# Two hybrid encoder layers on one core: the opening's order of loads, and the layer-0 modulation divided between TensorE and VectorE

## The chip, the cores and the metric

One Trainium2 chip, one core. The time is device microseconds of the launch, as the median of several runs; smaller is better. The trace is of one profiled execution. TensorE (PE) multiplies, VectorE (DVE), ScalarE (ACT) and GpSimd (POOL) work elementwise, and SyncE (SP) issues most transfers.

## What is computed

Two consecutive layers on x of 512 tokens by 1024 channels, in float32. Everything before the layers' first projection matters here:

```python
c_act = jax.nn.silu(c)
for l in range(DEPTH):
    mod = c_act @ w_ada[l] + b_ada[l]
    shift, scale, gate = jnp.split(mod, 3, axis=-1)
    h = _rmsnorm(x, norm_w) * (1.0 + scale[:, None]) + shift[:, None]
    proj = h @ w_in
...
    x = x + gate[:, None] * (merged @ w_out[l])
```

The projection feeds a windowed attention, a pooling branch and a state-space branch, whose sum goes through w_out; a final RMSNorm ends the program. Shift and scale of layer 0 take 2048 of the 3072 columns of `c_act @ w_ada[0]`.

## The kernel before

Channels lie on partitions: xT, h and the products are 8 tiles of 128 channels by 512 tokens (k = 0 to 7). Each weight tile is 1024 by 128. A float32 product is made of three rounded ones: the tile is split into a high part (`w_hi`, on ScalarE) and a low part (`w_lo`, on GpSimd), h likewise (h_hi on ScalarE, h_lo on VectorE), and TensorE adds hi*hi, hi*lo and lo*hi for each k: 24 products of 128x128 by 128x512 for one weight tile, all with float32r operands. The order on each engine is written out by hand, and engines wait for each other through counting semaphores. SyncE issues transfers in program order, so a transfer queued behind a waiting one waits too.

The opening does the following, all of it in layer 0.

- **Transfers** (`sync`, L304 on): c, then the first quarter of w_ada (`quarter(0)`, L308 to L317), the four blocks of x, two weight tiles of w_in, and then by turns quarters 1, 2 and 3 and the other weight tiles. A quarter is 256 columns of shift and 256 of scale for all 1024 rows: eight transfers of 256 KB into one of two buffers, zs for quarters 0 and 2, big for 1 and 3. Weight tiles go whole, 512 KB each. Small tables (biases, norms, conv weights; `s_rows`) are issued by ScalarE (L899 to L903).
- **Modulation** (VectorE, `use_quarter`, L1139 to L1151): for each of eight row blocks k, the 128x512 slab times silu(c) of that block, added to a sum in psC1. The eighth goes to `quarter_acc`. TensorE then adds over the partitions (`quarter_sums`, L589 to L595, a product with a vector of ones for each 128 columns), and `quarter_mod` adds bias and makes the gain.
- **x**: TensorE transposes it block by block (`x_rows`, L579 to L587), VectorE or ScalarE copies it to xT; ScalarE squares it, VectorE forms the inverse root, and TensorE copies that over all partitions (`spread`, L568 to L573).
- **h**: quarter q gives h tiles 2q and 2q+1: `h_32` (VectorE), `h_high` (ScalarE), `h_low` (VectorE), one after the other.
- **Wide part** (TensorE, `wide_part`, L613 to L624, and the list after L626): five weight tiles (`WIDE`: the three pairs' first five) are multiplied side by side in five PSUM banks, two k at a time, as h tiles appear. After it come small tables and the sixth tile, and from then on weight tiles two by two.

Of the kernel before, what the change touches and what calls it, by code (L numbers as in the profile page):

```python
# [103 lines left out]
def build(nc, x, c, w_ada, b_ada, norm_w, w_in, rel_bias, attn_sinks, pool_w, pool_scale, conv_w, conv_b, dt_bias,  # L104
# [11 lines left out]
    with ExitStack() as ctx:  # L116
# [75 lines left out]
        s_rawx = [sem(f"raw_wide_loaded{i}") for i in range(4)]  # L192
# [13 lines left out]
        s_adau = sem("ada_used")  # L206
        s_adam, s_mod = sem("ada_summed"), sem("mod_done")
# [65 lines left out]
        quarter_acc = [buf_d[:, 0:512], buf_d[:, 512:1024]]  # L273
        quarter_ps = [main[1]] + [psB[:, 512:1024]] * (QUARTERS - 1)
# [14 lines left out]
        def part_count(l, u, half):  # L289

            return (l * COUPLES + u) * 2 + half + 1

        def wait_raw(eng, l, u, b):
            if is_wide(l, u):
                eng.wait_ge(s_rawx[2 * u + b - 2], 16)
            else:
                eng.wait_ge(s_raw[b], (l * COUPLES + u + 1 - (2 if l + u > 0 else 0)) * 16)
# [7 lines left out]
        def _(sp):  # L305
            sp.dma_start(stage_e[0:KT, :], c.rearrange("b (a p) -> (b a) p", p=P)).then_inc(s_crow, 16)

            def quarter(q):  # L308

                n = D // QUARTERS  # L310
                for g in range(KT // 2):
                    if q >= 2:
                        sp.wait_ge(s_adau, (q - 2) * KT + 2 * g + 2)
# [11 lines left out]
            def load(l, u, b, w, col, kt=KT):  # L325
                if is_wide(l, u):
                    sp.dma_start(w_bufs(l, u, b)[0], w[l, :, :, col:col + P]).then_inc(s_rawx[2 * u + b - 2], 16)
                    return
                sp.wait_ge(s_split[b], part_count(0, 0, 1) if (l, u) == (0, 3) else (l * COUPLES + u) * 2)
                sp.dma_start(raw[:, b, 0:kt, :], w[l, :, 0:kt, col:col + P]).then_inc(s_raw[b], 16)  # L330

            def wide(i):
                load(0, i // 2, i % 2, w_in_t, i * P + COL_Q)

            quarter(0)
# [31 lines left out]
            for l in range(DEPTH):  # L367
# [63 lines left out]
                def next_slab(l, half, k):  # L431
                    n = half * KT + k
                    if l + 1 < DEPTH:
                        sp.wait_ge(s_yz, (l + 1) * PAIRS)
                        if n >= 4:
                            sp.wait_ge(s_adau, QUARTERS * KT + n - 3)
# [18 lines left out]
        def _(pool):  # L455
# [20 lines left out]
            def split_half(l, u, b, half, kt=KT):  # L476
                raw_b, hi_b, lo_b = w_bufs(l, u, b)
                cut = slice(half * BT_, (half + 1) * BT_)
                pool.wait_ge(s_hi[b], part_count(l, u, half) if kt == KT else (l * COUPLES + u) * 2 + 2)
# [12 lines left out]
            for l in range(DEPTH):  # L492
                for u in range(U_GA + 1):
                    split(l, u, 0)
                    split(l, u, 1)
# [20 lines left out]
        def _(pe):  # L516
# [18 lines left out]
            def tile_part(l, u, b, k0, k1, ready):  # L535
# [3 lines left out]
                for k in range(k0, k1):  # L539
                    pe.wait_ge(s_split[b], part_count(l, u, k // BT_))  # L540
# [37 lines left out]
            pe.wait_ge(s_rows, 16 * N_ROWS)  # L578
# [961 lines left out]
```

## Time and profile before

| | |
|---|---|
| median of 3 runs | 1195.08 us (1193.89 to 1195.45) |
| the profiled execution | 1194.21 us |
| its span in the trace | 1192.5 us |
| TensorE busy | 1145.6 us, 96% of the span |
| VectorE, ScalarE, GpSimd busy | 628.8, 514.0, 519.5 us |
| moved by DMA | 139.22 MB |

The span leaves out what lies around the program in the measured time (1.7 us here). The chain of waits follows back, from the last instruction, what released each step; the timeline lists instructions with start and duration. TensorE's durations overlap: the distance between two starts is what one costs in a row of them.

### The profile page before, as it was taken

The page shows a single profiled execution, that of the slowest core. Times are in us where ns is not written, and L with a number is a line of the kernel's source. Part 1 is how long each engine was busy: PE and PEld are TensorE (multiplying, and loading weights), DVE is VectorE, ACT ScalarE, POOL GpSimd, SP SyncE. Part 2 cuts the span into 40 slices and gives each one's busy share as a digit, 9 for nine tenths or more (in the row PEclk, how much of TensorE's full clock was granted, in tenths as well). Part 3 has the DMA queues.
Part 4 walks back from the last instruction along what each step waited for, and adds up shares of the span by engine and source line. Part 5 has one row for each costly group of instructions (what it writes and reads, how often), then busy time and mean ns, then how long its engine had stood idle before and what let it go on. Part 6 is the DMA issues. An engine that isn't in the chain of part 4 may idle for free.

```text
span 1192.5 us, 15180 instructions
## 1 busy us (share of the span) xinstructions
PE 1145.6 (96%) x5882; PEld 939.5 (79%) x5882; DVE 628.8 (53%) x759; ACT 514.0 (43%) x879; POOL 519.5 (44%) x381
## 2 busy tenths in 40 slices
PE   4899999999999999999979999999999999999997
PEld 3678888878888888887867788888888887788876
DVE  5806256568786554445340444555877753132274
ACT  4235256755445523224233534656444553232322
POOL 2334534434334446554514463434343425455441
PEclk9899999999999999999979999999999999999998
DMA  9745523335433455543313462332634422433332
GB/s 301 201 100 168 168 58 89 89 99 129 115 107 82 132 170 157 155 129 105 109 35 98 133 214 72 90 88 69 162 88 107 122 73 80 115 100 95 92 93 81
DMA packets 222200, 139.22 MB, mean 117 GB/s; under 512 B 11912, under 2 KB 212656, under 8 KB 222128
## 3 DMA queue, kind: packets, MB, share of 16 engines
q1 hardware_dynamic: 221480, 137.59, 40.5%
q8 instruction: 47, 0.77, 0.3%
q10 hardware_dynamic: 648, 0.66, 0.2%
q14 instruction: 25, 0.20, 0.1%
HBM read 135.08 MB, written 2.62 MB: 115 GB/s over the span
## 4 chain that ended last, share of the span: by engine, by line
PE 85%; DVE 5%; DMA 4%; POOL 2%; ACT 1%; SPq 1%; issue 1%; DVEq 0%; ACTq 0%
PE main L519 74%; DMA raw<-in_w_in 4%; PE psC L519 3%; PE psA L519 3%; PE psB L519 2%; POOL w_lo L480 2%; DVE h_lo L1463 1%; DVE xbc L1418 1%; ACT w_hi L864 1%; SPq L428 1%; DMA xbc<-in_x 1%; PE psB L674 1%; PE psB L694 0%; DVE psC L1150 0%; DVE misc L1298 0%
## 5 line engine op out<-in xcount | busy, mean ns | idle before, releaser
L480 POOL TENSOR_TENSOR w_lo<-raw,w_hi 128x512 fp32r<-128x512 f32 x352 | 503.9, 1454 | 639.1 <-ACT w_hi L864 639.1
L519 PE MATMUL main<-h_hi,w_hi 128*128 128x512 f32 x1152 | 461.1, 400 | 16.0 <-POOL w_lo L480 7.4
L519 PE MATMUL main<-h_hi,w_lo 128*128 128x512 f32 x1152 | 450.8, 391 | 0.0
L519 PE MATMUL main<-h_lo,w_hi 128*128 128x512 f32 x1152 | 450.7, 391 | 0.0
L864 ACT ACTIVATE w_hi<-raw 128x512 fp32r<-128x512 f32 x352 | 204.2, 625 | 343.2 <-PE main L519 247.8
L519 PEld LDWEIGHTS main<-h_hi,w_hi 128*128 128x128 f32 x1152 | 217.6, 189 | 75.8 <-issue 25.6
L519 PEld LDWEIGHTS main<-h_hi,w_lo 128*128 128x128 f32 x1152 | 217.6, 189 | 46.6
L519 PEld LDWEIGHTS main<-h_lo,w_hi 128*128 128x128 f32 x1152 | 217.8, 189 | 45.0 <-issue 1.9
L1452 DVE TENSOR_TENSOR tmp<-main,misc 128x512 f32<-128x512 f32 x32 | 22.1, 691 | 174.8 <-PE main L519 171.1
L1298 DVE SCALAR_TENSOR_TENSOR misc<-main,cols,misc 128x511 f32<-128x511 f32 (+2 forms) x96 | 71.9, 749 | 65.1 <-ACT misc L864 62.5
L519 PE MATMUL main<-y_hi,w_hi 128*128 128x512 f32 x256 | 101.3, 396 | 0.0
L519 PE MATMUL main<-y_lo,w_hi 128*128 128x512 f32 x256 | 99.7, 389 | 0.0
L519 PE MATMUL main<-y_hi,w_lo 128*128 128x512 f32 x256 | 99.7, 389 | 0.0
L864 ACT ACT_TABLE_LOAD x69 | 88.5, 1283 | 2.0 <-PEq L1526 0.8
L864 ACT ACTIVATE misc<-main 128x512 f32<-128x512 f32 x48 | 28.6, 597 | 139.1 <-PE main L519 139.0
L519 PEld LDWEIGHTS main<-y_hi,w_hi 128*128 128x128 f32 x256 | 48.1, 188 | 10.8 <-issue 1.4
L519 PEld LDWEIGHTS main<-y_hi,w_lo 128*128 128x128 f32 x256 | 48.1, 188 | 10.2
L519 PEld LDWEIGHTS main<-y_lo,w_hi 128*128 128x128 f32 x256 | 48.1, 188 | 9.5
L1272 DVE SCALAR_TENSOR_TENSOR xbc<-xbc,fcol 128x1024 f32<-128x1024 f32 x16 | 26.8, 1674 | 27.2 <-DMA xbc<-in_w_ada 27.1
L1454 DVE TENSOR_TENSOR big<-big,tmp 128x512 f32<-128x512 f32 x32 | 38.8, 1213 | 1.1
L864 ACT ACTIVATE misc<-main,cols 128x512 f32<-128x512 f32 x32 | 24.6, 769 | 25.5 <-PE main L519 25.5
L1242 DVE TENSOR_SCALAR tmp<-psC,hpar 16x512 f32<-16x512 f32 x2 | 1.5, 740 | 62.4 <-PE psC L519 62.4
(225 smaller groups left out, 1078.4 us busy)
## 6 DMA issues: line engine op xcount, KB each, us to landing
raw<-in_w_in SPq DMA_DIRECT2D x128, 512.0 KB, 3.8
xbc<-in_w_ada SPq DMA_DIRECT2D x16, 512.0 KB, 4.8
zs<-in_w_ada SPq DMA_DIRECT2D x16, 512.0 KB, 4.7
raw<-in_w_pc SPq DMA_DIRECT2D x16, 512.0 KB, 3.8
raw<-in_w_out SPq DMA_DIRECT2D x16, 512.0 KB, 3.7
zs<-in_w_ada SPq DMA_DIRECT2D x16, 256.0 KB, 5.6
big<-in_w_ada SPq DMA_DIRECT2D x16, 256.0 KB, 6.2
tmp<-step_rows SPq DMA_DIRECT2D x8, 512.0 KB, 4.1
```

Source lines behind the costliest of these rows:

```text
L428: sp.dma_start(buf_w[e * CHUNK:(e + 1) * CHUNK, :].rearrange("q (i n) -> q i n", n=PAIR), bass.AP(tensor=exp_rows.tensor, offset=first, ap ...
L480: nc.gpsimd.tensor_tensor(lo_b[:, cut, :], raw_b[:, cut, :], hi_b[:, cut, :].bitcast(F32), ALU.subtract).then_inc(s_split[b], 2 * BT_ // kt)
L519: return nc.tensor.matmul(o, a, b_, start=start, stop=stop)
L674: last = nc.tensor.transpose(psB[:, h * P:(h + 1) * P], buf_d[:, h * P:(h + 1) * P], ident[:, :])
L864: return nc.scalar.activation(o, i, func, **kw)
L1242: ch.link(ts_(v, psC0[0:SH, :], hpar[:, 0, l:l + 1], None, ALU.add))
L1272: stt(gate_acc, gate_slab[b], fcol[:, ds(j * 2 + b, 1)], gate_acc, ALU.mult, ALU.add).then_inc(s_gsu[b], 1)
L1298: ins = stt(cvb[:, b, back:SEQ], main[b][:, 0:SEQ - back], lcol[:, col_at(p * 4 + (V_CW + tap * CT + i))], cvb[:, b, back:SEQ], ALU.mult, ...
L1418: last = stt(xbc[:, i, tok], xbc[:, i, tok], gskip[:, i:i + 1], y_sum[:, i * P:(i + 1) * P], ALU.mult, ALU.add)
L1452: tt(buf_r[:, 0:512], main[1][:, :], gate, ALU.mult).then_inc(s_evac[1], 1)
L1454: tt(at(merged, m), at(merged, m), buf_r[:, 0:512], ALU.add).then_inc(s_acc, 1)
L1463: tt(at(h_lo, k), at(merged, k), at(h_hi, k).bitcast(F32), ALU.subtract).then_inc(s_m, 1)
```

## The change

Seven edits, all in the opening of layer 0 (the other hunks renumber semaphores).

1. SyncE sends the four blocks of x first, then quarter 0.
2. The five wide weight tiles go in halves of 256 KB (k 0 to 3 of all five between quarters 0 and 1, k 4 to 7 of all five between quarters 1 and 2). The sixth follows quarter 3. Quarter 2 waits for TensorE's use of quarter 0 instead of VectorE's.
3. Quarters 0 and 2 are formed on TensorE (`quarter_rows`): silu(c) of row block k, one column, is stationary, the 128x512 slab moves, and eight such float32 products add up a row of 512 in PSUM. ScalarE copies the row (`row_copy`), and four products with a one turn it into columns (`quarter_cols`). VectorE keeps quarters 1 and 3.
4. TensorE transposes all of x before quarter 0; it waits for the small tables after two of the four blocks, not before the first.
5. The wide part runs over five tiles at once in each of its four passes (before: four, with the fifth put in behind the sums).
6. The eight products of quarter 2 stand in the second pass, four behind the second weight tile and four behind the fourth.
7. ScalarE and GpSimd split the wide tiles by halves in the order in which they arrive.

```diff
-                        sp.wait_ge(s_adau, (q - 2) * KT + 2 * g + 2)
+                        sp.wait_ge(s_adar if q == 2 else s_adau, 2 * g + 2)
...
+            def wide(half):
+                cut = slice(half * BT_, (half + 1) * BT_)
+                for i, (u, b) in enumerate(WIDE):
+                    sp.dma_start(w_bufs(0, u, b)[0][:, cut, :], w_in_t[0, :, cut, i * P:(i + 1) * P]
+                                 ).then_inc(s_rawx[i + 6 * half], 16)
             for t in range(PAIRS):
                 sp.dma_start(stage_x[:, t, :], x_t[:, t, :]).then_inc(s_xrow[t], 16)
+            quarter(0)
             wide(0)
+            quarter(1)
             wide(1)
-            quarter(1)
-            wide(2)
-            wide(3)
             quarter(2)
-            wide(4)
             quarter(3)
-            wide(5)
+            sp.dma_start(w_bufs(0, 2, 1)[0], w_in_t[0, :, :, 5 * P:6 * P]).then_inc(s_rawx[5], 16)
...
+                if l == 0:
+                    for half in range(2):
+                        for u, b in WIDE:
+                            split_half(l, u, b, half)
+                    split(l, 2, 1)
+                for u in range(U_GA if l == 0 else 0, U_GA + 1):
...
-            pe.wait_ge(s_rows, 16 * N_ROWS)
...
+            row_ps = [psC1[0:1, :], psB[0:1, 512:1024]]
+            def quarter_rows(q, k0, k1):
+                for k in range(k0, k1):
+                    pe.wait_ge(s_ada[q % 2 * 4 + k // 2], (q // 2 + 1) * 32)
+                    mm(row_ps[q // 2], fcol[:, k:k + 1], quarter_slab[q % 2][:, k], k == 0, k == KT - 1
+                       ).then_inc(s_adar, 1)
+            def quarter_cols(q):
+                pe.wait_ge(s_arow, q // 2 + 1)
+                for j in range(QUARTERS):
+                    last = mm(quarter_ps[q][:, q * QUARTERS + j:q * QUARTERS + j + 1],
+                              quarter_row[q // 2][:, j * P:(j + 1) * P], ones[0:1, 0:1])
+                last.then_inc(s_adam, 1)
...
             x_rows(0)
+            x_rows(1)
+            pe.wait_ge(s_rows, 16 * N_ROWS)
             for l in range(DEPTH):
                 nc.tensor.transpose(psC0[:, l * P:l * P + V_ROWS], stage_v[0:V_ROWS, l, :],
                                     ident[0:V_ROWS, 0:V_ROWS])
             nc.tensor.transpose(psC0[:, 2 * P:2 * P + 2 * KT], stage_e[0:2 * KT, :],
                                 ident[0:2 * KT, 0:2 * KT]).then_inc(s_rT, 1)
-            quarter_sums(0)
-            for t in range(1, PAIRS):
-                x_rows(t)
+            x_rows(2)
+            x_rows(3)
+            pe.wait_ge(s_cact, 1)
+            quarter_rows(0, 0, 6)
             pe.wait_ge(s_cols, 2)
             spread(psC0, rms, 1)
-            for i in range(2):
+            quarter_rows(0, 6, 8)
+            quarter_cols(0)
+            for i in range(5):
+                if i == 2:
+                    pe.wait_ge(s_xc, PAIRS)
                 wide_part(i, 0, 2)
-            pe.wait_ge(s_xc, PAIRS)
             quarter_sums(1)
-            for i in range(2, 4):
-                wide_part(i, 0, 2)
-            for i in range(4):
+            for i in range(5):
                 wide_part(i, 2, 4)
-            quarter_sums(2)
-            wide_part(4, 0, 4)
-            for i in range(4):
+                if i == 1:
+                    quarter_rows(2, 0, 4)
+                if i == 3:
+                    quarter_rows(2, 4, 8)
+            quarter_cols(2)
+            for i in range(5):
                 wide_part(i, 4, 6)
-            quarter_sums(3)
-            wide_part(4, 4, 6)
+                if i == 2:
+                    quarter_sums(3)
             for i in range(5):
                 wide_part(i, 6, 8)
...
+            def row_copy(i):
+                act.wait_ge(s_adar, (i + 1) * KT)
+                f(quarter_row[i], (psC1[0:1, :], psB[0:1, 512:1024])[i], ACT.Copy).then_inc(s_arow, 1)
+            row_copy(0)
             for b in range(2):
                 w_hi_half(0, 0, b, 0)
             h_high(0, 0)
             h_high(0, 1)
-            for b in range(2):
-                w_hi_half(0, 0, b, 1)
-            w_hi_part(0, 1, 0)
-            w_hi_part(0, 1, 1)
+            for u, b in WIDE[2:]:
+                w_hi_half(0, u, b, 0)
+            for u, b in WIDE[:4]:
+                w_hi_half(0, u, b, 1)
             h_high(0, 2)
             h_high(0, 3)
-            w_hi_part(0, 2, 0)
+            w_hi_half(0, 2, 0, 1)
+            row_copy(1)
             h_high(0, 4)
             h_high(0, 5)
...
             dve.wait_ge(s_cact, 1)
-            for k in range(KT):
-                use_quarter(0, k)
             x_copy(0)
+            x_copy(1)
+            inverse_root(rms, s_xsq, PAIRS, 1, sm[:, 4])
             dve.wait_ge(s_rT, 1)
             nc.vector.tensor_copy(cols[:, :, :], psC0[:, 0:2 * P].rearrange("p (l n) -> p l n", l=DEPTH)
                                   [:, :, 0:V_ROWS]).then_inc(s_cols, 1)
             nc.vector.tensor_copy(fcol[:, KT:2 * KT], psC0[:, 2 * P + KT:2 * P + 2 * KT]).then_inc(s_cols, 1)
+            x_copy(2)
             dve.wait_ge(s_cols, 2)
-            x_copy(1)
-            quarter_mod(0)
-            x_copy(2)
-            inverse_root(rms, s_xsq, PAIRS, 1, sm[:, 4])
-            for q in range(QUARTERS):
-                if q > 0:
-                    for k in range(0 if q == 1 else 2, KT):
-                        use_quarter(q, k)
-                    if q < QUARTERS - 1:
-                        for k in range(2):
-                            use_quarter(q + 1, k)
-                    quarter_mod(q)
+            def two_tiles(q):
+                quarter_mod(q)
                 if q == 0:
                     dve.wait_ge(rms[3], 1)
                     dve.wait_ge(s_xc, PAIRS)
...
                 h_32(0, 2 * q + 1)
                 h_low(0, 2 * q)
                 h_low(0, 2 * q + 1)
+            two_tiles(0)
+            for k in range(KT):
+                use_quarter(1, k)
+            two_tiles(1)
+            for k in range(2):
+                use_quarter(3, k)
+            two_tiles(2)
+            for k in range(2, KT):
+                use_quarter(3, k)
+            two_tiles(3)
```

TensorE, the program's start, up to the first product of the wide part. In these rows `zs,fcol` is slab by silu(c), `ident,xbc` a transpose of x, `ones,tmp` the sums or the turn into columns, `ident,sm` the spread of the inverse root, `w_hi` and `w_lo` a weight tile. Before:

```order
L585 MATMUL psA<-ident,xbc 128x128 x8
L628 MATMUL psC<-ident,big 128x124 x2
L630 MATMUL psC<-ident,big 128x16
L519 MATMUL main<-ones,tmp 128x1 x4
L585 MATMUL psB<-ident,xbc 128x128 x8
L585 MATMUL psA<-ident,xbc 128x128 x8
L585 MATMUL psB<-ident,xbc 128x128 x8
L519 MATMUL psC<-ident,sm 128x128 x4
L519 MATMUL main<-h_hi,w_hi 128x512
```

The same place in the changed kernel:

```order
L593 MATMUL psA<-ident,xbc 128x128 x8
L593 MATMUL psB<-ident,xbc 128x128 x8
L655 MATMUL psC<-ident,big 128x124 x2
L657 MATMUL psC<-ident,big 128x16
L593 MATMUL psA<-ident,xbc 128x128 x8
L593 MATMUL psB<-ident,xbc 128x128 x8
L527 MATMUL psC<-zs,fcol 1x512 x6
L527 MATMUL psC<-ident,sm 128x128 x4
L527 MATMUL psC<-zs,fcol 1x512 x2
L527 MATMUL main<-ones,tmp 128x1 x4
L527 MATMUL main<-h_hi,w_hi 128x512
```

Eight products of 1x512 now stand between the transposes and the columns, the spread among them.

TensorE in the wide part's second pass, where it goes from tile 1 (bank main) to tile 2 (bank psA). Here `y_hi` and `y_lo` are the split parts of wide tiles 2 to 4. Before:

```order
L519 MATMUL main<-h_hi,w_hi 128x512
L519 MATMUL main<-h_lo,w_hi 128x512
L519 MATMUL main<-h_hi,w_lo 128x512
L519 MATMUL psA<-h_hi,y_hi 128x512
L519 MATMUL psA<-h_lo,y_hi 128x512
```

The same place in the changed kernel:

```order
L527 MATMUL main<-h_hi,w_hi 128x512
L527 MATMUL main<-h_lo,w_hi 128x512
L527 MATMUL main<-h_hi,w_lo 128x512
L527 MATMUL psB<-zs,fcol 1x512 x4
L527 MATMUL psA<-h_hi,y_hi 128x512
L527 MATMUL psA<-h_lo,y_hi 128x512
```

Four products of quarter 2 stand between the two tiles; the other four stand between psA and psB of the same pass.

VectorE, from h tiles 0 and 1 to the modulation of tiles 2 and 3. `tmp<-xT` is h_32, `psC<-big` and `psC<-zs` are uses of a slab, `mod<-psB` is `quarter_mod`. Before:

```order
L1178 SCALAR_TENSOR_TENSOR tmp<-xT,mod,psC 128x512 x2
L1182 SCALAR_TENSOR_TENSOR h_lo<-tmp,mod,h_hi 128x512 x2
L1146 TENSOR_SCALAR psC<-big,fcol 128x512
L1150 SCALAR_TENSOR_TENSOR psC<-big,fcol,psC 128x512 x6
L1150 SCALAR_TENSOR_TENSOR tmp<-big,fcol,psC 128x512
L1146 TENSOR_SCALAR psC<-zs,fcol 128x512
L1150 SCALAR_TENSOR_TENSOR psC<-zs,fcol,psC 128x512
L1167 TENSOR_TENSOR mod<-psB,cols 128x2x2
```

In the changed kernel:

```order
L1217 SCALAR_TENSOR_TENSOR tmp<-xT,mod,psC 128x512 x2
L1221 SCALAR_TENSOR_TENSOR h_lo<-tmp,mod,h_hi 128x512 x2
L1186 TENSOR_SCALAR psC<-big,fcol 128x512
L1189 SCALAR_TENSOR_TENSOR psC<-big,fcol,psC 128x512 x6
L1189 SCALAR_TENSOR_TENSOR tmp<-big,fcol,psC 128x512
L1206 TENSOR_TENSOR mod<-psB,cols 128x2x2
```

The eight uses of quarter 1 stay where they were; the two of quarter 2 behind them are gone.

## Rows read from the trace of the kernel before

**Rows 1.** The page: span, busy times, chain by engine.

```profile
span 1192.5 us, 15180 instructions
...
PE 1145.6 (96%) x5882; PEld 939.5 (79%) x5882; DVE 628.8 (53%) x759; ACT 514.0 (43%) x879; POOL 519.5 (44%) x381
...
PE 85%; DVE 5%; DMA 4%; POOL 2%; ACT 1%; SPq 1%; issue 1%; DVEq 0%; ACTq 0%
```

**Rows 2.** The chain of waits in the opening: start us, us, what.

```profile
22.88 1.14 PE psC L519 x8
...
33.82 1.84 PE psB L519 x8
35.65 5.13 PE psA L519 x12
...
43.55 2.72 PE psA L519 x12
...
55.64 0.86 PE psB L519 x8
56.50 0.02 issue
...
59.36 3.02 PE main L519 x12
...
66.45 1.44 PE psC L519 x34
```

**Rows 3.** GpSimd's and TensorE's timelines up to the wide part's start.

```profile
2.56 2.84 POOL L472 TENSOR_SCALAR_AFFINE_SELECT seg<-seg 128x128 f32<-128x128 f32 x8
...
14.33 0.62 PE L628 MATMUL psC<-ident,big 124*128 124x124 f32 x2
...
15.09 1.87 PE L519 MATMUL main<-ones,tmp 128*128 128x1 f32 x8
...
18.56 1.71 PE L585 MATMUL psA<-ident,xbc 128*128 128x128 f32 x8
20.24 1.06 PE L585 MATMUL psB<-ident,xbc 128*128 128x128 f32 x8
...
26.48 0.52 PE L519 MATMUL main<-h_hi,w_hi 128*128 128x512 f32 x1 [2.48 <-DVE h_lo L1182]
...
31.02 0.39 PE L519 MATMUL main<-h_hi,w_lo 128*128 128x512 f32 x1
```

**Rows 4.** ScalarE's queue in the DMA view of 11 to 12 us.

```profile
q10 hardware_dynamic: 2, 0.00, 0.1%
```

**Rows 5.** TensorE's timeline around one float32 product of 512 columns.

```profile
274.80 1.02 PE L519 MATMUL psC<-misc,poolw 128*128 128x512 f32 x2
...
275.88 0.39 PE L519 MATMUL main<-h_lo,w_hi 128*128 128x512 f32 x1
```

**Rows 6.** ScalarE: a copy of 512 elements out of PSUM.

```profile
61.03 0.60 ACT L864 ACTIVATE big<-main 128x512 f32<-128x512 f32 x1 [0.43 <-PE main L519]
```

**Rows 7.** VectorE's timeline: slab products and the h tiles between them.

```profile
12.15 0.75 DVE L1150 SCALAR_TENSOR_TENSOR tmp<-zs,fcol,psC 128x512 f32<-128x512 f32 x1
...
26.92 0.75 DVE L1146 TENSOR_SCALAR psC<-big,fcol 128x512 f32<-128x512 f32 x1
...
33.78 0.75 DVE L1146 TENSOR_SCALAR psC<-zs,fcol 128x512 f32<-128x512 f32 x1
...
35.69 0.16 DVE L1167 TENSOR_TENSOR mod<-psB,cols 128x4 f32<-128x4 f32 x1 [0.30 <-PE psB L519]
...
38.95 4.18 DVE L1150 SCALAR_TENSOR_TENSOR psC<-zs,fcol,psC 128x512 f32<-128x512 f32 x5
```

**Rows 8.** Stretches: PE, PEld, DVE, ACT, POOL busy; granted clock, DMA, GB/s.

```profile
28.00:30.00 2.00, 1.71 (x4) 0.83 (x3) 1.79 (x3) 1.36 (x3) 2.00 (x3) 0.50 1.13 325
...
36.00:38.00 2.00, 2.00 (x6) 1.52 (x5) 1.83 (x4) 1.13 (x2) 0.00 (x0) 0.50 1.13 330
...
58.00:60.00 2.00, 0.64 (x3) 0.50 (x4) 1.74 (x3) 1.98 (x3) 0.00 (x0) 1.00 0.00 0
```

More of the change, by code:

```diff
@@ L191, in build @@
         s_raw, s_split = sem2("raw_loaded"), sem2("w_split")
-        s_rawx = [sem(f"raw_wide_loaded{i}") for i in range(4)]
+        s_rawx = [sem(f"raw_wide_loaded{i}") for i in range(11)]
         s_hi = sem2("w_hi_done")
@@ L287, in w_bufs, with part_count, wait_raw @@
             return raw[:, b], w_hi[:, b], w_lo[:, b]
-        def part_count(l, u, half):
+        def part_count(l, u, half, b):
+            if l == 0 and u < U_GA:
+                return u + 1 + (3 - b) * half if (u, b) != (2, 1) else 5 + half
             return (l * COUPLES + u) * 2 + half + 1
-        def wait_raw(eng, l, u, b):
-            if is_wide(l, u):
-                eng.wait_ge(s_rawx[2 * u + b - 2], 16)
+        def wait_raw(eng, l, u, b, half):
+            if l == 0 and u < U_GA:
+                eng.wait_ge(s_rawx[2 * u + b + (6 * half if (u, b) != (2, 1) else 0)], 16)
             else:
-                eng.wait_ge(s_raw[b], (l * COUPLES + u + 1 - (2 if l + u > 0 else 0)) * 16)
+                eng.wait_ge(s_raw[b], (l * COUPLES + u - 2) * 16)
         gate_slab = [xbc[:, 2 * i:2 * i + 2, :].rearrange("p a b -> p (a b)") for i in range(2)]
@@ L589, in quarter_sums @@
             def quarter_sums(q):
[L591 removed]
+                pe.wait_ge(s_adau, (q + 1) // 2 * KT)
                 for j in range(QUARTERS):
[L593 removed]
+                    last = mm(quarter_ps[q][:, q * QUARTERS + j:q * QUARTERS + j + 1], quarter_acc[q // 2][:, j * P:(j + 1) * P],
                               ones[:, 0:1])
                 last.then_inc(s_adam, 1)
+            row_ps = [psC1[0:1, :], psB[0:1, 512:1024]]
[10 more added lines that the diff above has]
+                last.then_inc(s_adam, 1)
             def half_sums(half):
[L598 removed]
+                pe.wait_ge(s_adau, 2 * KT + (half + 1) * KT)
                 for j in range(KT):
@@ L869, in w_hi_half @@
                     act.wait_ge(s_tile[b], 1 if (l, u) == (0, 3) else l * COUPLES + u)
-                wait_raw(act, l, u, b)
+                wait_raw(act, l, u, b, half)
                 k = half * BT_
@@ L1142, in use_quarter @@
                 part = quarter_slab[q % 2][:, k]
-                if q + k > 0:
-                    dve.wait_ge(s_adau, q * KT + k)
                 if k == 0:
+                    if q == 1:
+                        dve.wait_ge(s_arow, 1)
+                    else:
+                        dve.wait_ge(s_adau, KT)
                     ts_(psC1, part, fcol[:, k:k + 1], None, ALU.mult).then_inc(s_adau, 1)
                     return
-                if k == KT - 1 and q >= 2:
-                    dve.wait_ge(s_adam, q - 1)
-                stt(psC1 if k < KT - 1 else quarter_acc[q % 2], part, fcol[:, k:k + 1], psC1, ALU.mult, ALU.add
+                dve.wait_ge(s_adau, q // 2 * KT + k)
+                stt(psC1 if k < KT - 1 else quarter_acc[q // 2], part, fcol[:, k:k + 1], psC1, ALU.mult, ALU.add
                     ).then_inc(s_adau, 1)
```

24 lines of the change are left out of this document (8 added, 16 removed).

## The prediction

> **What bounds the kernel now.** First the page: TensorE is busy for 1145.6 of 1192.5 us and makes 85% of the chain of waits, VectorE 5% [rows 1]. So a microsecond is won where TensorE still stands, or where it is given less to do, and any product added to a stretch in which it never stands is paid in full. Then the chain in the opening, which is all that the change touches [rows 2]: what the reader should see is where it leaves TensorE. Up to 33.7 us it runs mostly through VectorE. From 33.82 to 56.5 us it is TensorE alone, product behind product; from 56.50 it goes for 2.86 us through VectorE and ScalarE to the product at 59.36; then TensorE alone again. The wide part begins at 26.48 [rows 3] and ends at 66.45, where the small tables begin [rows 2]. Behind that the order on TensorE is unchanged, so I take the time to move by as much as that end moves.
>
> Last, the stretches [rows 8]. The clock granted to TensorE was 0.50 (1.2 GHz) at 28 to 30 and 36 to 38 us. Before the first of these TensorE had waited for 2.48 us [rows 3], before the second from 31.4 (31.02 + 0.39 [rows 3]) to 33.82 us. At 58 to 60 us, after the 2.86 us without a product, it was still 1.00 (2.4 GHz).
>
> **Prices.** A float32r product of 512 columns costs 2.72/12 = 0.227 us at the full clock and 5.13/12 = 0.43 at half [rows 2]. A float32 product of 512 columns is two pieces. Its first starts at 274.80. Behind it stands one float32r product, and the one after that starts at 275.88; less that one's 0.23 this leaves 274.80 to 275.65: 0.85 us [rows 5]. The sums of a quarter, four float32 products of one column, cost 0.86 us at full clock and 1.84 at half [rows 2]; the turn of a row into columns is four such products and gets the same price.
>
> A 512-column product with one stationary column does not occur before. Its bounds: 0.227, the float32r product of as many columns, and 1.7, the row of 0.85 at half the clock. I take 0.85, since type and number of moving columns are the same there and what differs is only how many columns stand still.
>
> - TensorE can start when GpSimd has its constants, at 2.56 + 2.84 = 5.4 us. Two blocks of x take 1.7 us each, the distance from 18.56 to 20.24: to 8.9 [rows 3].
> - Then the wait for the small tables, which before was hidden. ScalarE's queue still moved packets between 11 and 12 us, none later [rows 4]. I take 11.5; if they came at once, 8.9. The transposes of tables take 0.76 (14.33 to 15.09): 12.3.
> - Two more blocks: 0.9 us each if the clock has risen (the last block took 1.06 with its end), 1.7 if not. In the trace the blocks became quick at 20.24, 7.6 us after the first work; counted from 5.4 that is 13. I take 0.9: 14.1 us.
> - Six row products, the spread (1.14 [rows 2]), two more: 6.8 + 1.1 = 8.0, to 22.1. The slabs are there by then: before, eight uses of quarter 0 ended before 12.9 us with nothing ahead of them, now 2 MB of x stand ahead, some 6 us at 330 GB/s [rows 8]: the last slab by 18, its product stands after 20.
> - ScalarE's copy of the row, 0.60 as its copy of 512 elements a partition [rows 6] (bounds 0.2 and 0.6), columns 0.86, and the way from there through the modulation and the three steps of an h tile, 2.86 (56.50 to 59.36 [rows 2]): 4.4 us with a gap of 0.1. **First wide product at 26.5**, against 26.48. No gain.
>
> The bounds of this are 23.9 (tables at once) and 37 (everything at half clock).
>
> **The wide part.** The same 120 products: 27.2 us. Added are the eight row products of quarter 2, 6.8 us; sums or columns follow each of three passes, 3 x 0.86 = 2.6. Against that VectorE is freed of eight uses, 6.86 us (26.92 to 33.78) [rows 7]. Is that worth something? Pass by pass, at full clock:
> 1. k 0 and 1 of five tiles, 6.8 us: to 33.3. VectorE ends tiles 0 and 1 at about 26.9 and quarter 1 at 33.7, as before. Wait 0.4, sums to 34.6.
> 2. Modulation and h tile 2: 2.8 us in which no product can run (56.50 to 59.36 is such a wait). Before, two wide tiles' products ran here; now all five tiles have had their turn ahead of the sums. To 37.4.
> 3. k 2 and 3, with the eight row products: 6.8 + 6.8, columns 0.9: to 51.9. The copy of the row is covered by the fifth tile's products.
> 4. Another 2.8 us of waiting, since the columns again stand behind everything: 54.7. VectorE, free since about 40, cannot shorten it: it waits for the columns.
> 5. k 4 and 5 of three tiles, 4.1: 58.8. VectorE has done two uses of quarter 3 early, and the other six after h tiles 4 and 5 (3.26 us, 35.69 to 38.95 [rows 7]): 52.0 + 3.3 + 6 x 0.857 = 60.4. Wait 1.6; sums and two tiles: 64.0.
> 6. h tile 6 is ready by then. k 6 and 7: 6.8 us, **end at 70.8**, against 66.45: 4.4 us later.
>
> What was taken off VectorE lay beside TensorE's work, what was put on TensorE lies on the path. GpSimd and ScalarE split the first halves of five tiles in time (tile 2 is due at 29, its low part at 27.7), the second halves are due only in pass 5. Quarter 1 has 5.5 MB ahead instead of 5.2, quarter 3 as much as before; at some 330 GB/s [rows 8] the difference is under 1 us and each is needed later than it was.
>
> **The clock.** The full clock in this sum is too kind. There are three waits of 2.8 us (before the first product, in 2 and in 4). Of three such waits in the trace two were followed by half clock, which cost 7 products x 0.2 = 1.4 us the first time and 12 x 0.2 plus the slower sums, 3.4 us, the second. I add one of each, less the 0.4 that the wait in pass 1 covers: 4.4 us. End at 75.2, **8.8 us later**. The profiled execution took 1194.21 us, 0.87 under the median of 1195.08; 1194.2 + 8.8 + 0.9 gives **1204**.
>
> **The rivals.** About 0.2%, 2.4 us, is what a measurement of this kernel can tell from no change: 1192.7 to 1197.5.
> - *Full clock throughout.* Row products fill TensorE's gaps ahead of the wide part, and the clock never falls. For it: 58 to 60 us at 1.00. Against: two of three. It takes the 4.4 us off again: 1199.5.
> - *The tables are early as well.* Start at 23.9, no half clock: end at 68.2, 1.8 us later: 1197. For it: the tables no longer share the engines with quarter 0 in its first microseconds. Against: x is moved at that time instead.
> - *One stationary column leaves the clock at half.* Nothing in the trace shows such a product. Then quarter 0's eight cost 13.6 and the spread twice, first product at about 35: 8 us more, 1212.
> - *Faster: the one-column product is cheap.* If it costs 0.23, sixteen are 10 us less, and the end falls to 65.2, 1194, and to 60.8, 1189, with the clock kept; I write 1191. The point from which it decides is 0.85 - 8.8/16 = 0.30 us a product. Against it stand the two pieces of 0.85 [rows 5]. The page named above would have it so.
>
> **How the numbers follow.** The sum with half clock in places: 0.50. Full clock: 0.20. Both together with early tables: 0.11. Half clock for the row products: 0.12. Cheap products: 0.07. Slower by over 0.2%: 0.50 + 0.20 + 0.12 = 0.82; within: 0.11; faster: 0.07. The range goes from the early tables, 1196.5, to 1210, which leaves out the cheap products and most of the half-clock case.
>
> **What would show it.** In the profile after: row products 0.85 us apart; the first wide product near 26; three waits of about 2.8 us on TensorE with h_lo as the releaser; the start of the small tables near 75 and not 66; the chain through TensorE in the second pass with row products in it. I am wrong if the tables' start is at or below 66.5, if the row products are clearly under 0.5 us, or if the time behind the opening changes by itself.

## The result and the profile after

The changed kernel takes 1208.98 us in the median of four runs (1204.66 to 1211.04), the kernel before 1195.26 us beside it. The ratio is 1.0109, with a 95% interval of 1.0076 to 1.0143: slower by some 13 us. Forecast were 1204, in a range from 1196.5 to 1210. The direction and the mechanism in the opening hold; the sum was too small by a third, and the range was met by 1 us only (a rerun of the same kernel, below, lies outside it). The profiled execution took 1210.58 us with a span of 1208.9, so its trace has to explain 16.4 us.

The page of the changed kernel, the lines that answer to [rows 1]:

```profile
span 1208.9 us, 15219 instructions
...
PE 1162.7 (96%) x5914; PEld 943.4 (78%) x5914; DVE 618.1 (51%) x743; ACT 513.9 (43%) x881; POOL 518.3 (43%) x381
...
PE 84%; DMA 5%; DVE 5%; ACT 2%; POOL 2%; issue 1%; SPq 1%; ACTq 0%; DVEq 0%
```

VectorE has 10.7 us less to do, TensorE 17.1 us more, and TensorE is where the chain runs. Its chain of waits in the opening (start us, us, what), to be laid beside [rows 2]:

```profile
16.00 8.15 PE psC L527 x24
...
24.17 0.59 ACT tmp L896
...
24.81 1.06 PE main L527 x8
...
29.10 4.59 PE main L527 x12
...
36.43 2.16 PE psB L527 x14
...
41.44 4.20 PE main L527 x12
45.64 3.88 PE psB L527 x8
49.53 2.92 PE psA L527 x12
52.45 6.10 PE psB L527 x22
...
61.40 5.46 PE main L527 x12
...
79.04 1.44 PE psC L527 x34
```

The reader sees the new rows in the expected order: the eight products of quarter 0 and the spread from 16.00 to 24.15, those of quarter 2 in two blocks of four (eight pieces) from 45.64 and at the start of the block at 52.45. The wide part ends at 79.04 and not at 66.45: 12.6 of the 16.4 us have come into being by then. The first wide product comes at 29.10 instead of 26.48 (+2.6), and the part from there to the end takes 49.9 us instead of 40.0 (+10.0).

TensorE's timeline at the start, beside [rows 3]:

```profile
7.24 1.80 PE L593 MATMUL psB<-ident,xbc 128*128 128x128 f32 x8
11.94 0.47 PE L655 MATMUL psC<-ident,big 124*128 124x124 f32 x2 [2.91 <-DMA big<-in_final_norm_w]
...
12.56 1.97 PE L593 MATMUL psA<-ident,xbc 128*128 128x128 f32 x8
14.32 1.67 PE L593 MATMUL psB<-ident,xbc 128*128 128x128 f32 x8
15.93 5.31 PE L527 MATMUL psC<-zs,fcol 128*1 128x512 f32 x12
...
29.10 0.62 PE L527 MATMUL main<-h_hi,w_hi 128*128 128x512 f32 x1 [3.25 <-DVE h_lo L1221]
```

The wait for the small tables is there (2.91 us, until 11.94), and the third and fourth block of x after it are slow: 1.76 us from start to start of the two, with a granted clock of 0.55 from 12 to 14 us and 0.60 from 14 to 16. Six row products then take 5.24 us, 0.87 each.

Stretches (busy us of PE, PEld, DVE, ACT, POOL, then granted clock, DMA share, GB/s), beside [rows 8]:

```profile
30.00:36.00 6.00, 6.00 (x22) 4.82 (x21) 5.27 (x8) 2.47 (x5) 6.00 (x6) 0.78 1.10 347
...
42.00:48.00 6.00, 6.00 (x16) 2.75 (x15) 1.38 (x2) 0.00 (x0) 1.11 (x1) 0.72 0.82 192
48.00:54.00 6.00, 6.00 (x20) 2.68 (x19) 0.00 (x0) 0.00 (x0) 0.00 (x0) 1.00 0.31 78
...
60.00:66.00 6.00, 4.60 (x11) 3.67 (x12) 5.04 (x8) 2.17 (x4) 2.57 (x2) 0.50 0.00 0
```

Two things stand in them. VectorE does nothing at all from 48 to 54 us; its own timeline gives it 15.09 us without work until TensorE's columns are there:

```profile
58.57 0.16 DVE L1206 TENSOR_TENSOR mod<-psB,cols 128x4 f32<-128x4 f32 x1 [15.09 <-PE psB L527]
```

It has been relieved of work in a stretch in which nobody waited for it. And after each of the three waits for an h tile (before 29.10, 41.44 and 61.40) the clock falls to 0.50 in some part of the stretch behind, at 60 to 66 us throughout.

### The profile page after: what moved, and what is told of

It reads as the page before. It is cut to its first block, busy times and chain, and to the rows that moved or that the text cites. A ratio compares the mean times of both kernels' runs of the same rounds, so it can differ in the third digit from the quotient of the medians.

```text
span 1208.9 us, 15219 instructions
## 1 busy us (share of the span) xinstructions
PE 1162.7 (96%) x5914; PEld 943.4 (78%) x5914; DVE 618.1 (51%) x743; ACT 513.9 (43%) x881; POOL 518.3 (43%) x381
## 4 chain that ended last, share of the span: by engine, by line
PE 84%; DMA 5%; DVE 5%; ACT 2%; POOL 2%; issue 1%; SPq 1%; ACTq 0%; DVEq 0%
PE main L527 72%; DMA raw<-in_w_in 5%; PE psC L527 4%; PE psA L527 3%; PE psB L527 3%; POOL w_lo L483 2%; DVE h_lo L1505 1%; DVE xbc L1460 1%; ACT w_hi L896 1%; SPq L431 1%; PE psB L706 1%; DMA big<-in_final_norm_w 1%; PE psB L726 0%; DVE misc L1340 0%; ACT h_hi L896 0%
## 5 line engine op out<-in xcount | busy, mean ns | idle before, releaser
L527 PE MATMUL main<-h_hi,w_hi 128*128 128x512 f32 x1152 | 463.2, 402 | 23.0 <-DVE h_lo L1221 11.5
L1494 DVE TENSOR_TENSOR tmp<-main,misc 128x512 f32<-128x512 f32 x32 | 22.1, 691 | 174.8 <-PE main L527 171.1
L527 PEld LDWEIGHTS main<-y_hi,w_hi 128*128 128x128 f32 x256 | 48.0, 188 | 10.8 <-issue 1.4
L1314 DVE SCALAR_TENSOR_TENSOR xbc<-xbc,fcol 128x1024 f32<-128x1024 f32 x16 | 28.0, 1751 | 26.7 <-DMA xbc<-in_w_ada 26.5
```

The lines of the kernel that those rows point to most:

```text
L527: return nc.tensor.matmul(o, a, b_, start=start, stop=stop)
L1314: stt(gate_acc, gate_slab[b], fcol[:, ds(j * 2 + b, 1)], gate_acc, ALU.mult, ALU.add).then_inc(s_gsu[b], 1)
L1494: tt(buf_r[:, 0:512], main[1][:, :], gate, ALU.mult).then_inc(s_evac[1], 1)
```

## The experiments

Each run was compared with the kernel before on the same chip. Below, "against before" is the ratio minus one, times 1195 us.

**The change again.** No edit.

> The changed kernel unchanged, for its spread and as the yardstick of the three runs beside it. If what followed the opening in its first trace (3.8 us more than before, behind the start of the small tables) is a matter of the clock's and GpSimd's chance, its median stays 11 to 15 us above before and its runs spread over 4 us or more; if it belongs to the change, the new trace shows the same 3.8 us again.

Measured: 1211.53 us (1208.64 to 1212.68), ratio 1.0135 (1.0121 to 1.0148), 16 us against before: above the 11 to 15 that I had expected, and above the upper bound of the prediction's range. The wide part ended at 81.22, and behind it 1129.5 us followed, 3.4 more than the 1126.1 of before. So that excess came again. It is taken up below.

**Seven of quarter 2's eight row products left out.** The modulation of h tiles 4 and 5 then holds only the first of eight row blocks of w_ada's third quarter.

```diff
-                if i == 1:
-                    quarter_rows(2, 0, 4)
                 if i == 3:
-                    quarter_rows(2, 4, 8)
+                    pe.wait_ge(s_ada[3], 64)
+                    mm(row_ps[1], fcol[:, 0:1], quarter_slab[0][:, 0]).then_inc(s_adar, 1)
```

> Seven of quarter 2's eight row products are left out (the modulation of h tiles 4 and 5 then holds one row block of eight). Theory 1, the products lie on TensorE's path at 0.87 us each: 6 us faster than the changed kernel, or 9 if the stretch at half clock covers some of them. Rival, VectorE or the slabs would have held TensorE there anyway: under 2 us faster, with a new wait for VectorE in pass 2 or 3.

Measured: 1203.97 us, ratio 1.0076 (1.0063 to 1.0088), 9 us against before where the change had 16: 7 us faster. Its chain in and behind pass 2:

```profile
41.35 3.00 PE main L527 x12
44.35 2.72 PE psA L527 x12
47.07 3.53 PE psB L527 x16
...
70.40 1.44 PE psC L527 x34
```

Pass 2 runs through without a wait for anybody, and the wide part ends at 70.40, 8.6 and 10.8 us before those of the two traces of the change. Theory 1 holds: seven products of 0.87 us are 6.1 us. The rest is in good part clock: here the wait of 2.87 us before 41.35 was not followed by half clock (granted clock 1.00 from 36 to 52 us), so the first tile of pass 2 took 3.00 us, and 4.20 and 5.45 in the two traces of the change. Why the clock stayed up this once is not shown.

**The tables' wait behind all of x.**

```diff
             x_rows(1)
+            x_rows(2)
+            x_rows(3)
             pe.wait_ge(s_rows, 16 * N_ROWS)
...
-            x_rows(2)
-            x_rows(3)
             pe.wait_ge(s_cact, 1)
```

> TensorE transposes all four blocks of x before it waits for the small tables. Theory 1, the 2.9 us wait for the tables at 9.0 to 11.9 us delays the row products of quarter 0 and all behind them: first row product at about 13.1 instead of 15.9, first wide product near 26.3 instead of 29.1, 2.8 us faster. Rival, quarter 0 has not landed by then: the products wait for the slabs and the gain is under 1 us.

Measured: 1208.92 us, ratio 1.011 (1.0094 to 1.0125), 13 us against before: 3 us faster than the change beside it. TensorE's timeline:

```profile
7.27 1.91 PE L593 MATMUL psB<-ident,xbc 128*128 128x128 f32 x8
8.97 1.19 PE L593 MATMUL psA<-ident,xbc 128*128 128x128 f32 x8
10.59 1.06 PE L593 MATMUL psB<-ident,xbc 128*128 128x128 f32 x8 [0.42 <-DVE xT L1227]
...
12.13 5.31 PE L527 MATMUL psC<-zs,fcol 128*1 128x512 f32 x12
...
25.31 0.76 PE L527 MATMUL main<-h_hi,w_hi 128*128 128x512 f32 x1 [3.25 <-DVE h_lo L1221]
```

Without the pause the third and fourth block take 1.19 and 1.06 us instead of 1.97 and 1.67, the row products start 3.8 us earlier, and the first wide product comes at 25.31. Quarter 0 had landed by 12.1, so the rival falls.

**Products of zeros in the three waits.**

```diff
+            def filler(n, start=False):
+                for _ in range(n):
+                    mm(main[0][:, 0:P], zero[:, :], xT[:, 0, 0:P], start, start)
...
             quarter_cols(0)
+            pe.wait_ge(s_xc, PAIRS)
+            filler(10, True)
...
             quarter_sums(1)
+            filler(10)
...
             quarter_cols(2)
+            filler(10)
```

> Ten float32 products of 128 columns with zeros (0.21 us each at full clock) stand in each of the three waits for h tiles 0, 2 and 4 and add nothing to the sums. Theory 2, the waits let the clock fall and that costs the kernel some 6 us (three stretches at 0.50 of 3.4, 3.4 and 6.8 us): granted clock 1.00 from 24 to 79 us, and 4 to 7 us faster. Rival, the clock falls for another reason or products of 128 columns do not hold it: same clock as before the fillers, time the same or up to 3 us slower.

Measured: 1205.51 us, ratio 1.0086 (1.0073 to 1.01), 10 us against before: 6 us faster than the change, by adding 30 products that compute nothing. Stretches of this run:

```profile
30.00:36.00 6.00, 6.00 (x28) 4.91 (x27) 5.27 (x8) 2.63 (x6) 6.00 (x6) 1.00 1.10 347
...
60.00:66.00 6.00, 4.43 (x24) 3.46 (x22) 4.25 (x6) 0.07 (x1) 2.23 (x2) 1.00 0.00 1
66.00:72.00 6.00, 6.00 (x22) 4.78 (x22) 3.15 (x6) 2.87 (x4) 0.00 (x0) 0.72 0.00 0
```

From 18 us on the clock stays at 1.00 up to 66 us. It falls once, in 66 to 72, after a wait of 1.57 us that carried no fillers, the one for the sums of quarter 3 (its sums stand at 65.25 in the chain). That the clock was lost in the three waits is shown by these rows, since nothing but their filling was changed. What it cost in the opening is shown less sharply: the wide part ended at 77.60, 1.4 and 3.6 us before the change's two traces, with the fall at 66 to 72 still in it. The larger part of the 6 us came behind the opening, where 1125.1 us followed instead of 1129.5; it is taken up below.

**Columns of quarter 2 ahead of two tiles.**

```diff
-                if i == 1:
+                if i == 0:
                     quarter_rows(2, 0, 4)
-                if i == 3:
+                if i == 1:
                     quarter_rows(2, 4, 8)
-            quarter_cols(2)
+                if i == 2:
+                    quarter_cols(2)
```

> Quarter 2's row products stand behind the first and second tile of pass 2 and the columns behind the third, so two tiles' products (2.7 us) cover the modulation and h tile 4. Theory 1 and 2: the wait before pass 3 (2.85 us) shrinks to 0.5 us or less, the clock keeps its full level there, and the kernel is 3 to 6 us faster than the changed one. Rival, VectorE's six uses of quarter 3, which begin 2.7 us earlier too, or late slabs of quarter 2 set the pace: under 1.5 us faster.

Measured: 1207.84 us, ratio 1.0115 (1.0098 to 1.0132), 14 us against before; beside the change's 1.0135 that is 2.4 us, between the two expectations. The wait before pass 3 is gone, but VectorE's six uses of quarter 3 then set the sums of pass 3 (66.93 in its chain), and the wide part ends at 79.23. It can't be told from the change's first measurement of 1.0109.

**Quarter 2 back on VectorE.** Quarter 0 stays on TensorE, x first and the halves stay (semaphore counts follow).

```diff
-                if i == 1:
-                    quarter_rows(2, 0, 4)
-                if i == 3:
-                    quarter_rows(2, 4, 8)
-            quarter_cols(2)
+                if i == 2:
+                    quarter_sums(2)
...
                 use_quarter(1, k)
+            for k in range(2):
+                use_quarter(2, k)
             two_tiles(1)
+            for k in range(2, KT):
+                use_quarter(2, k)
             for k in range(2):
                 use_quarter(3, k)
```

> Quarter 2 goes back to VectorE (sums behind the third tile of pass 2), quarter 0 stays on TensorE, everything else as changed. Theory 1, moving quarter 2 to TensorE was the costliest part: end of the wide part 6 to 8 us earlier than in the changed kernel, 1202 to 1205 us. Rival, VectorE becomes the bound with 8 more products (6.9 us): a wait for the sums of quarter 2 appears that is as long as what was won, and the time stays within 2 us of the changed kernel.

Measured: 1200.1 us, ratio 1.005 (1.0032 to 1.0069), 6 us against before, 10 us faster than the change in its rerun. The chain:

```profile
47.71 1.38 PE psA L527 x6
49.10 0.80 PE psB L527 x8
...
58.26 1.05 PE psB L527 x8
...
69.25 1.44 PE psC L527 x34
```

Now VectorE is in the chain from 49.9 to 58.26, as the rival said, and it is still far cheaper: the wide part ends 9.8 and 12.0 us before that of the change's two traces, more than the 6 to 8 of theory 1. The costliest part of the change is found: giving quarter 2 to TensorE. Not all of it is the products. In this run the sums stand behind the third tile, two tiles' products cover the modulation and h tile 4, and TensorE's wait of 2.87 us before pass 3 is gone with them; the run with the columns ahead of two tiles took away that wait alone, the one without seven products the products alone. Against the change's first measurement (1.0109) the gain is 7 us and not 10.

**Both, quarter 2 on VectorE and the tables last.** The two edits together.

> Quarter 2 on VectorE and the wait for the small tables behind all four blocks of x, together; quarter 0 on TensorE, x first and the halves stay. If the two prices add (8 to 9 us and 2.6), the first wide product comes near 25.5 us and the time is within 2 us above that of the kernel before. Rival, VectorE's chain from the first h tile on is what bounds the rest: it starts 3 us earlier than in the run with quarter 2 alone, and all of that arrives at the end of the wide part too, which ends at 66 to 67 us. If instead the slabs or GpSimd hold, less than 1.5 us arrives.

Measured: 1196.45 us, ratio 1.0034 (1.0021 to 1.0047), 4 us against before. The first wide product came at 25.74 and the wide part ended at 65.53, 0.9 us before that of the kernel before. What the opening had lost is won back; 4 us are missing still, twice what I had allowed, and they lie behind it: 1130.8 us follow instead of 1126.1.

**Both, and products of zeros.** Twelve before the first wide product, ten before pass 2.

```diff
             quarter_cols(0)
+            pe.wait_ge(s_xc, PAIRS)
+            filler(12, True)
...
             quarter_sums(1)
+            filler(10)
```

> The same with products of zeros in the waits for h tiles 0 and 2, to hold the clock. Theory 2: clock 1.00 up to 60 us and 1 to 3 us faster than the run without them. Rival, as in the kernel before with such products: VectorE never stands still after its first h tile and bounds the wide part, so under 1 us changes. This is the version that could beat the kernel before; I expect it within 2 us of it.

Measured: 1190.83 us (1189.55 to 1193.58, twelve runs), ratio 0.9985 with an interval of 0.9975 to 0.9995. This version beats both kernels, the one before by some 2 us. Its first wide products and a stretch:

```profile
22.42 2.94 PE L529 MATMUL main<-xT,zero 128*128 128x128 f32 x24
25.75 0.47 PE L529 MATMUL main<-h_hi,w_hi 128*128 128x512 f32 x1 [0.38 <-DVE h_lo L1228]
```

```profile
36.00:42.00 6.00, 4.76 (x22) 3.44 (x20) 5.45 (x8) 1.63 (x3) 1.35 (x1) 1.00 1.11 346
42.00:48.00 6.00, 4.61 (x23) 3.61 (x24) 5.48 (x11) 2.35 (x4) 0.37 (x1) 1.00 0.84 199
```

The clock is 1.00 in every stretch from 16 to 78 us, and the wide part ends at 63.84. I had expected this one within 2 us of before, and so it came. Against the run without the zeros it is 6 us faster, more than either expectation (1 to 3, under 1): the clock held, and VectorE, busy 5.45 of 6 us, bounds the middle of the wide part, yet 1.7 us came off its end, and 7 us lie behind it.

**The kernel before with x first.** Only the order of the loads.

```diff
-            quarter(0)
             for t in range(PAIRS):
                 sp.dma_start(stage_x[:, t, :], x_t[:, t, :]).then_inc(s_xrow[t], 16)
+            quarter(0)
```

> The kernel before with nothing changed but the order of the loads: x ahead of quarter 0. TensorE's order has the sums of quarter 0 behind the first block of x, and VectorE's uses of quarter 0 come ahead of the copies of x, so x first cannot be used before quarter 0 has landed, 3 to 5 us later than now: first wide product 2 to 4 us later, time 0 to 4 us above before. If x's transfer was what bounded the start, it would be faster by over 1 us instead.

Measured: 1196.87 us, ratio 1.0033 (1.0021 to 1.0045), 4 us slower. TensorE's timeline:

```profile
11.44 1.94 PE L585 MATMUL psA<-ident,xbc 128*128 128x128 f32 x8 [8.80 <-DMA big<-in_final_norm_w]
...
18.32 1.86 PE L519 MATMUL main<-ones,tmp 128*128 128x1 f32 x8 [4.31 <-DVE tmp L1150]
...
29.90 0.77 PE L519 MATMUL main<-h_hi,w_hi 128*128 128x512 f32 x1 [2.47 <-DVE h_lo L1182]
```

As expected: TensorE waits 4.31 us for quarter 0, and the first wide product is 3.4 us later. The first block of x waits until 11.44 for the tables, not for x.

**The kernel before with products of zeros**, nine before the first wide product, nine before the sums of quarter 1, five before pass 4, by the same `filler`.

> The kernel before, with products of zeros in its waits (nine of 128 columns before the first wide product, nine before the sums of quarter 1, five before pass 4). Theory 2, half clock at 26.8 to 30.2 and 33.6 to 40.4 us came from those waits and cost some 4 us: granted clock 1.00 from 20 to 70 us and 2 to 4 us faster than before. Rival, the stretch after 33.8 is then bound by VectorE's six uses of quarter 2: clock up but under 1 us gained.

Measured: 1195.19 us, ratio 1.0006 (0.9993 to 1.0019): no change. The wide part ended at 65.27, 1.2 us earlier, with VectorE in the chain up to 48.8. The rival holds.

**The kernel before with tile 2 ahead of the sums of quarter 1.**

```diff
             pe.wait_ge(s_xc, PAIRS)
+            wide_part(2, 0, 2)
             quarter_sums(1)
-            for i in range(2, 4):
-                wide_part(i, 0, 2)
+            wide_part(3, 0, 2)
```

> The kernel before, with wide tile 2's first two row blocks ahead of the sums of quarter 1 instead of behind them. Theory 1, TensorE's wait from 31.4 to 33.8 us is filled by 1.4 to 2.6 us of products that must be done anyway: 1.4 us faster, and 3 to 4 if the clock stays up as well. Rival, tile 2's low part (GpSimd, due at 31.9) comes late, or VectorE bounds what follows: within 1 us of before.

Measured: 1192.48 us, ratio 0.9993 (0.9978 to 1.0007): not told from no change. The wide part ended at 66.51. The filled wait only moved: TensorE then waited 1.85 us for h tile 2 before 39.05, and the clock fell there.

**Both of these.** Tile 2 ahead, nine products of zeros before the first wide product and two before tile 2.

> The kernel before with tile 2 ahead of the sums of quarter 1, nine products of zeros before the first wide product and two before tile 2. If clock and filled wait add, the clock stays at 1.00 from 20 us on and the time is 2 to 3 us below before. If VectorE is the bound by then (it never stands still from its first h tile on in the kernel before with such products), it stays within 1.5 us of before, as each of the two edits did alone.

Measured: 1197.14 us, ratio 1.0029 (1.0016 to 1.0042), 3.5 us slower, a miss of both expectations. The clock did not stay up either: behind a wait of 1.84 us before 38.56 it was 0.67 and then 0.50 from 38 to 42 us. The wide part ended at 66.08, a little earlier than before. All of the loss lies behind it, where 1129.0 us followed.

**What lies behind the opening.** From the end of the wide part to the end of the span the traces show 1126.1 us for the kernel before, 1129.9 and 1129.5 for the change, 1130.7 with the tables last, 1125.1 with products of zeros, 1131.8 without seven row products, 1128.8 with the columns early, 1128.4 with quarter 2 on VectorE, 1130.8 with that and the tables last, 1123.8 for the fastest version, and 1125.3, 1127.3, 1124.2 and 1129.0 for the four variants of the kernel before. The order of instructions there is the same in all. In the change's first trace the chain at this place is

```profile
117.95 2.24 DVE xbc L1314
120.20 0.35 SPq L367
120.60 5.95 DMA raw<-in_w_in
...
128.77 27.50 PE main L527 x120
```

SyncE's load of a weight tile stood behind a slab of gate columns that VectorE freed late, and landed 5.95 us after that. But TensorE had other products to run meanwhile; by its own timeline it stood for 0.84 us:

```profile
128.77 0.47 PE L527 MATMUL main<-h_hi,w_hi 128*128 128x512 f32 x1 [0.84 <-POOL w_lo L483]
```

In the kernel before the chain is TensorE's alone at this place, from 88.14 to 142.72, and there is no such wait. A larger part is clock. Some 30 us later TensorE waits 0.78 us for ScalarE, in the change (157.03) as in the kernel before (143.46) and in the run with fillers (154.84). The stretch from 160 to 164 us, first in the change:

```profile
160.00:164.00 4.00, 4.00 (x54) 3.42 (x54) 1.58 (x3) 0.00 (x0) 0.00 (x0) 0.50 0.46 131
```

The same in the run with fillers:

```profile
160.00:164.00 4.00, 4.00 (x20) 3.29 (x19) 2.42 (x6) 0.00 (x0) 0.00 (x0) 1.00 0.28 81
```

From that wait to the end of the next 72 products it takes 23.7 us in the change (157.03 to 180.69), 22.1 in the kernel before (143.46 to 165.56) and 20.6 with fillers (154.84 to 175.48). So 1.6 of the change's 3.8 us, and 3.0 of the 4.4 that the fillers won behind the opening, arise here. Why a wait of one length is followed by half clock in one trace and by the full one in another is not shown.

The clock also goes with the spread within one kernel. Of the 23 executions of the kernel before beside the last runs the shortest (1190.68 us) had a mean granted clock of 0.983 and the longest (1196.28) 0.979; of the twelve of the variant with tile 2 ahead and zeros those of 1192.62 and 1199.91 us had 0.990 and 0.983. Executions of one kernel thus lie as far apart as most of these remainders do, so that a remainder of 1124 or 1130 us in a single trace is not shown to belong to its version. What sets the rest stays open.

## Why the prediction was right, and where its sum failed

**Right.** The row product: 0.85 us taken, 0.87 measured (5.24 us for six). The wait for the tables: from 8.9 to 11.5 taken, 9.0 to 11.94 measured. That quarter 2 on TensorE lies on the path and its eight uses on VectorE did not: leaving seven products out gave 7 us back, moving all eight to VectorE, with the wait behind them, 7 to 10. The three waits for h tiles 0, 2 and 4, with h_lo as releaser: there. TensorE's clock under products with one stationary column: it held, and the rival of half clock for them falls. So do the rivals of full clock throughout (0.50 from 60 to 66 us) and of early tables (11.94). The rival of cheap products falls with the 0.87; so does what the Trainium skill's page "TensorE: Matmul & The Clock Gate", section "Back-to-back issue gap", would have made of them. The section names no type of operand; its 0.22 us is near the 0.227 of a float32r product here and far from float32.

**The start of the wide part: 26.5 taken, 29.10 and 30.15 measured.** The failed step is "Two more blocks: 0.9 us each". I let the clock rise 7.6 us after the first work, as in the trace of before, and left out that TensorE would stand for 2.9 us in between. The blocks took 1.76 and 1.61 us, 1.6 us more in all. With the pause taken away they took 1.6 us (0.42 of it a wait) and 1.0 us, and the row products began at 12.13. The way from the end of the columns to the first product took 3.25 us where I had put 2.86, and the copy of the row with its two hand-overs 0.68 us.

**The clock: the failed step is "Of three such waits two were followed by half clock".** I read 56.50 to 59.36 in the chain as 2.86 us in which TensorE ran no product. The chain shows what released the last step, not what else TensorE did. Behind the sums at 55.64 it ran six products of the fifth tile, and TensorE's own timeline gives its wait:

```profile
59.36 0.47 PE L519 MATMUL main<-h_hi,w_hi 128*128 128x512 f32 x1 [1.37 <-DVE h_lo L1182]
```

So the trace of before had two waits of 2.4 us or more in or just before the wide part, both followed by half clock, and one of 1.37 that was not. All three waits of the change (3.25, 2.87 and 2.87 us) were followed by it. Read rightly, the rows would have said three of three, not two.

In size the term came out nearly right all the same, by luck: it had two falls of 2.2 us on average, and what came were three of 1.1 to 1.5. The part from the first wide product to the end took 49.9 us in the change, 51.1 in its rerun, and 48.3 with the fillers (29.26 to 77.60). In that last run products behind the fall at 66 us were still slow: from the sums to pass 4 it took 5.4 us where my sum had 3.6. Without these 1.8 us the part is 46.5 us at full clock, an estimate from that one run. So the clock cost 3.4 us in the one trace and 4.6 in the other, against 4.4 taken.

**The same part at full clock: 44.3 us taken, some 46.5 found.** The terms that were too small are many and each is small: the products of pass 2 with the eight of quarter 2 and its columns 15.55 us for 14.5, the wait for h tile 2 3.33 for 2.8, VectorE's stretch 8.8 for 8.5, the first pass with its sums 8.3 for 8.1, the fourth 6.94 for 6.8 (all from the run with fillers).

**Behind the opening: "I take the time to move by as much as that end moves".** The end moved by 12.6 us and the span by 16.4. This is the third step that failed: the other 3.8 us were put at nothing, with the unchanged order of instructions as the only reason. The prediction had named a change of time behind the opening as a sign of being wrong, and by that sign it was. The runs show that this remainder varies by some 8 us (1123.8 to 1131.8) between versions whose instructions there are the same; in the change 1.6 us of it are half clock behind 157 us and 0.8 the wait before 128.77, and the rest is not explained.

Together: the sum had 44.3 us and 4.4 for the clock behind a start at 26.5, for an end at 75.2. Measured was 79.04: 2.6 of the 3.8 us are the late start, 1.2 lie in the wide part, and another 3.8 us behind the opening. The chances leant rightly on slower. The range held by luck: its upper bound of 1210 lies 1 us above the first measurement and 1.5 below the rerun (1211.53), and its upper half was used up in part by a place that the sum did not look at.

## What to carry to other kernels

- Before work is moved from an idle engine to a busy one, look in the chain of waits at which of the two is there. Eight uses of a slab take 6.9 us of VectorE, which stood still for 15 us in that stretch of the change; seven products for the same slab cost TensorE, which did not stand still there, 6.1 us of path and the kernel 7.
- A wait on TensorE is not only its own length. From the wait for the first h tile to the end of the wide part, 23 of the 24 waits of 1.8 us or more in these traces were followed by half clock; the 24th was the 2.87 us before 41.35 in the run without seven products. In between both came: half clock after 1.60, 1.57 and 1.44 us (the last before 37.23 with x first in the kernel before), none after the 1.57 before 22.88 in the kernel before. No wait of 1.40 or less was followed by it there, and one of 0.78 was, further on (157.03 in the change). Products that add zeros held the clock over such waits. In the opening that brought 1.4 to 3.6 us where TensorE was the bound; in the kernel before it took 1.2 us off the wide part and nothing off the time, and VectorE was in the path there.
- A pause in a chain is read from the engine's own timeline, with the idle time in its brackets, and never from the chain alone: 2.86 us in the chain were 1.37 of TensorE standing, and a transfer of 5.95 us was 0.84.

## What the hardware showed that I had not expected

- Transposes alone brought the full pace: with the tables last, TensorE had done nothing since 5.5 us but transposes of x, and the distance from block to block fell from 1.7 us to one block in 1.06 by 10.59. The granted clock reads 1.00 in all of that stretch, slow blocks included, so the rise is read from the pace alone. A pause of 2.9 us at the same place kept them slow for 4 us more.
- Products with a single stationary column held the full clock for 8 us on end (16.0 to 24.1, granted clock 1.00), the spread among them. In the rerun, where the transposes ahead of them were slow to the end, the first six took 5.8 us instead of 5.2, and the last two 1.9 as here.
- The small tables, 0.13 MB issued by ScalarE until 6.2 us, landed at 11.2 to 12.0 us whatever else was sent first: quarter 0 (q10's last packets at 11 to 12 us, [rows 4]) or x (11.19, with quarter 2 on VectorE, to 12.01 in the rerun).
